# First expert's gate: two column pieces multiplied with all tokens, the place matrix scaled and in f32

## What is computed

```
def _expert_choice_ffn(xn, router_w, w_gate, w_up, w_down):
    probs = softmax(xn @ router_w)                 # 256 tokens x 16 experts
    gate, idx = top_k(probs^T, 32)                 # each expert takes its 32 best tokens
    xg = xn[idx]                                   # 16 experts x 32 tokens x 1024
    h = silu(xg @ w_gate) * (xg @ w_up)            # 1024 -> 2048
    y = (h @ w_down) * gate                        # 2048 -> 1024
    return zeros.at[idx].add(y)                    # back to the tokens
```

## Time and profile before

| | |
|---|---|
| median of three runs | 2114.65 us |
| the profiled execution | 2118.86 us |
| its span, first to last instruction | 2117.0 us |
| mean granted TensorE clock | 0.859 |
| HBM traffic, mean over the span | 348 GB/s |
| busy: PE, DVE, ACT, POOL | 77%, 35%, 21%, 15% |

### The profile page before, as it was taken

The page is one execution under the profiler, slowest core; times in us unless marked ns, Lnnn a source line. Parts: engine busy times, 40 slices in busy tenths (PEclk is TensorE's granted clock), DMA queues, the critical chain, the costliest instruction groups (busy, mean ns, idle before and its releaser), DMA issues. The chain is left out here.

```text
span 2117.0 us, 23616 instructions
## 1 busy us (share of the span) xinstructions
PE 1626.3 (77%) x9071; PEld 779.3 (37%) x9071; DVE 738.2 (35%) x1697; ACT 449.9 (21%) x992; POOL 315.6 (15%) x312
## 2 busy tenths in 40 slices
PE   7998879979777877789889766666666666766665
PEld 7987855545333333339678311111111110111110
DVE  4265267776777767654653200000000000000001
ACT  4255134222222312224531300000000000000001
POOL 0141033433433333310040000000000000000000
PEclk9998989989999999999989886778777777787777
DMA  7541389999999999986204899999999999999997
GB/s 267 170 128 61 130 327 379 419 420 421 419 421 421 420 420 421 421 340 239 110 14 174 357 420 420 419 420 420 421 421 420 420 421 421 421 420 420 421 420 313
DMA packets 111668, 737.54 MB, mean 348 GB/s; under 512 B 14048, under 2 KB 15968, under 8 KB 27616
## 3 DMA queue, kind: packets, MB, share of 16 engines
q1 hardware_dynamic: 74432, 467.86, 54.7%
q0 software_dynamic: 36864, 268.45, 30.6%
q10 hardware_dynamic: 288, 0.08, 0.0%
HBM read 735.30 MB, written 1.05 MB: 348 GB/s over the span
## 5 line engine op out<-in xcount | busy, mean ns | idle before, releaser
L2501 PE MATMUL ps<-arena,xe 128*32 128x512 f32 x2032 | 376.7, 832 | 194.2 <-DMA arena<-in_experts_in 194.2
L1123 PE MATMUL ps<-arena 128*128 128x512 f32 x820 | 404.1, 643 | 114.7 <-ACT arena L1302 114.6
L2658 DVE TENSOR_TENSOR low<-low,ps 128x512 f32<-128x512 f32 x16 | 11.0, 688 | 873.2 <-PE ps L2501 873.2
L1508 DVE CUSTOM_DVE_ANT_0 arena<-arena,ps 128x1024 f32<-128x1024 f32 x205 | 247.7, 1218 | 126.4 <-DMA arena<-in_peer,arena 126.3
L1123 PEld LDWEIGHTS ps<-arena 128*128 128x128 f32 x820 | 163.4, 205 | 336.4 <-issue 192.0
L1023 POOL DMA_INDIRECT arena<-in_peer,arena x205 | 196.2, 957 | 435.1 <-PE ps L1123 334.8
L2501 PEld LDWEIGHTS ps<-arena,xe 128*32 128x32 f32 x2032 | 47.3, 124 | 509.8 <-DMA arena<-in_experts_in 487.9
L2525 PE MATMUL ps<-arena,hT 128*32 128x512 f32 x1024 | 163.9, 743 | 78.6 <-DMA arena<-in_experts_down 67.4
L2690 POOL TENSOR_TENSOR low<-h,hT 128x512 f32<-128x512 f32 x2 | 2.5, 1270 | 933.8 <-DVE h L2671 933.8
L1302 ACT ACTIVATE arena<-ident,arena 128x128 f32<-128x128 f32 x256 | 83.7, 391 | 149.5 <-DVE arena L1518 145.2
L2525 PEld LDWEIGHTS ps<-arena,hT 128*32 128x32 f32 x1024 | 26.1, 122 | 198.9 <-DMA arena<-in_experts_down 160.7
(11 more groups left out here) (459 smaller groups left out, 1937.8 us busy)
## 6 DMA issues: line engine op xcount, KB each, us to landing
arena<-in_experts_in SPq DMA_DIRECT2D x254, 1024.0 KB, 26.9
arena<-in_experts_down SPq DMA_DIRECT2D x128, 1024.0 KB, 27.2
ring<-in_stream SPq DMA_DIRECT2D x42, 512.0 KB, 5.4
arena<-in_stream SPq DMA_DIRECT2D x36, 512.0 KB, 3.8
arena<-in_stream SPq DMA_DIRECT2D x14, 1024.0 KB, 7.1
arena<-in_peer,arena POOLq DMA_INDIRECT x205, 18.4
h<-in_x SPq DMA_DIRECT2D x1, 1024.0 KB, 5.0
arena<-in_sel SPq DMA_DIRECT2D x1, 1024.0 KB, 5.7
```

What stands on the lines that cost most here:

```text
L1123: last = nc.tensor.matmul(ps[:, 4 + 2 * t + half, :], diag[:, n % DIAGS, :], slot(n)[:, D + half * BANK:D + (half + 1) * BANK], start=firs ...
L1508: nc.vector.tensor_tensor_reduce(slot(n)[:, 0:D], slot(n)[:, 0:D], xrow(j // (QUADS // NT)), 1.0, 0.0, ALU.mult, ALU.add, act_in[:, u % 2, ...
L2501: last = nc.tensor.matmul(ps[32 * j:32 * (j + 1), 4 + r // KB, :], xe[:, k, :], w[:, j * BANK:(j + 1) * BANK], start=(k == 0), stop=(k == ...
```

## The change

Expert 0's gate matrix is partly stored in column pieces (all 1024 rows x 256 columns, as [128, 8 x 256]) in place of row pieces. The order of its pieces is now: gate column pieces 0 and 1, the eight row pieces of up, gate column pieces 2 to 7. The eight down pieces and all other experts stay as they were.

- Gate column pieces 0 and 1 are multiplied with all 256 tokens (`for_all_tokens`, from `hT`), one quarter ahead of the turn of the probabilities, three behind it. ACT copies the result (256 tokens x 512 columns) to `dense` when both pieces are used, and `open_chosen` picks expert 0's 32 rows with a product with `onehot`.
- `onehot` is f32 and holds the token's 1/rms in place of 1; `xs`, `xs_parts` and the split by ACT and POOL are gone. The gathers multiply the residual `h` itself, in f32: two products a k in place of four.
- DVE makes expert 0's 32 columns of `onehot` first (`oh_first`), PE gathers expert 0 by itself (16 products of 128x32 into bank 0), and one DVE instruction brings them to `xe`. The other 15 experts' gathers (8 x 2 products of 128x480) stand between up pieces (four) and behind gate pieces 2 to 5 (four).
- Gate column pieces 2 to 7 (`open_gate`): each is 8 products of 32 stationary and 256 moving columns, all into one column group (`j = c // 2`).
- Piece 15, still in `hT`, is now loaded behind piece 18, when two pieces are used.

```diff
             for q in range(RING3 + 2, PAIR):
                 sync.wait_ge(ring.used, ring.before(q) + 1)
+                if q == RING3 + 1 + DENSE:
+                    first_lap(RING3 - 1)
                 load(q, 0)
...
+            def for_all_tokens(c, t):
+                if t == 0:
+                    ring.arrived(pe, c)
+                w = ring.piece(c, 0).rearrange("p (k c) -> p k c", k=KB)
+                for k in range(KB):
+                    last = nc.tensor.matmul(ps[:, 2 + c, t * S:(t + 1) * S], hT[:, k, t * P:(t + 1) * P], w[:, k, :],
+                                            start=(k == 0), stop=(k == KB - 1))
+                if t == NT - 1:
+                    last.then_inc(ring.used, 1)
+
+            for_all_tokens(0, 0)
             pe.wait_ge(ex_p, 1)
...
             last.then_inc(pt_ps, 1)
+            for_all_tokens(0, 1)
+            for t in range(NT):
+                for_all_tokens(1, t)
             pe.wait_ge(rep_ready, 1)
...
+            pe.wait_ge(oh_first, NT)
+            for k in range(KB):
+                for t in range(NT):
+                    last = nc.tensor.matmul(ps[:, 0, k * CAP:(k + 1) * CAP], h[:, t, k * P:(k + 1) * P], onehot[:, t, 0:CAP],
+                                            start=(t == 0), stop=(t == NT - 1))
+            last.then_inc(x0_ps, 1)
...
                 for t in range(NT):
-                    for a in range(2):
-                        last = nc.tensor.matmul(ps[:, k % 4, :], xs_parts[:, a, t, k * P:(k + 1) * P], onehot[:, t, :],
-                                                start=(t == 0 and a == 0), stop=(t == NT - 1 and a == 1))
+                    last = nc.tensor.matmul(ps[:, k % 4, CAP:NEXP * CAP], h[:, t, k * P:(k + 1) * P], onehot[:, t, CAP:NEXP * CAP],
+                                            start=(t == 0), stop=(t == NT - 1))
                 last.then_inc(xg_ps, 1)
...
+            def open_up(k):
+                if k == 0:
+                    pe.wait_ge(xe_first, 1)
+                q = DENSE + k
+                ring.arrived(pe, q)
+                w = ring.piece(q, 0)
+                for j in range(4):
+                    last = nc.tensor.matmul(ps[32 * j:32 * (j + 1), 5, :], xe[:, k, :], w[:, j * BANK:(j + 1) * BANK],
+                                            start=(k == 0), stop=(k == KB - 1), tile_position=(0, 32 * j))
+                last.then_inc(ring.used, 1)
+
+            def open_chosen():
+                for t in range(NT):
+                    nc.tensor.matmul(ps[0:32, 4, :], onehot[:, t, 0:CAP].bitcast(F32), dense[:, t, :],
+                                     start=(t == 0), stop=(t == NT - 1), tile_position=(0, 0))
+
+            def open_gate(c):
+                q, j, half = KB + c, c // 2, c % 2
+                ring.arrived(pe, q)
+                w = ring.piece(q, 0).rearrange("p (k c) -> p k c", k=KB)
+                for k in range(KB):
+                    last = nc.tensor.matmul(ps[32 * j:32 * (j + 1), 4, half * S:(half + 1) * S], xe[:, k, :], w[:, k, :],
+                                            start=(k == 0), stop=(k == KB - 1), tile_position=(0, 32 * j))
+                last.then_inc(ring.used, 1)
...
+                    for k in range(KB):
+                        open_up(k)
+                        if k % 2 == 1:
+                            gather(k // 2)
+                    open_chosen()
+                    for c in range(DENSE, KB):
+                        open_gate(c)
+                        if c < DENSE + 4:
+                            gather(c - DENSE + 4)
```

More of the change, by code:

```diff
@@ L1694 @@
 FIRST_LOADS = 4
+DENSE = 2
 OUT_BANK, POOLED_EARLY = (6, 7, 2, 3), 2
@@ L2331, in experts @@
     low_c, over_xs, over_hT = Carve(low2), Carve(low2), Carve(hT[:, :, :].rearrange("p k s -> p (k s)"))
-    xs = low_c(NT, D)
+    low_c(2 * D)
     xg = low_c(KB, NEXP * CAP)
-    r_tile = lambda name, *shape: expert_stack.enter_context(nc.sbuf_tensor(name, [P, *shape], F32R))
-    onehot = r_tile("onehot", NT, NEXP * CAP)
-    xs_parts = r_tile("xs_parts", 2, NT, D)
+    onehot = expert_stack.enter_context(nc.sbuf_tensor("onehot", [P, NT, NEXP * CAP], F32))
     diag = expert_stack.enter_context(nc.sbuf_tensor("diag", [NEXP, NEXP, CAP], F32R))
@@ L2487, in expert @@
             def expert(pair, odd, opening=False, closing=False):
                 e = pair * 2 + odd
-                if not opening:
+                if opening:
+                    for k in range(KB):
[7 more added lines that the diff above has]
+                            gather(c - DENSE + 4)
+                    pe.wait_ge(xg_sb, KB)
+                else:
@@ L2490, in expert @@
                     pe.wait_ge(xe_ready, e)
-                for r in range(2 * KB):
+                for r in range(0 if opening else 2 * KB):
                     q = odd * PER + r
[L2494 to L2497, removed]
                     ring.arrived(pe, q, pair)
@@ L2566, in _, with hidden @@
             nc.scalar.activation(probs[:, :, :], probs[:, :, :], ACT.Exp).then_inc(ex_exp, 1)
+            act.wait_ge(ring.used, DENSE)
             for t in range(NT):
-                nc.scalar.activation(xs[:, t, :], h[:, t, :], ACT.Copy, scale=rms[:, 1, t:t + 1]).then_inc(xs_all, 1)
-                act.wait_ge(xs_all, t + 1)
-                nc.scalar.activation(xs_parts[:, 0, t, :], xs[:, t, :], ACT.Copy).then_inc(xs_high, 1)
+                nc.scalar.activation(dense[:, t, :].rearrange("p (c s) -> p c s", c=DENSE), ps[:, 2:2 + DENSE, t * S:(t + 1) * S],
+                                     ACT.Copy).then_inc(dense_sb, 1)
             for k in range(KB):
                 act.wait_ge(xg_ps, k + 1)
[L2573 to L2576, removed]
+                nc.scalar.activation(xg[:, k, CAP:NEXP * CAP], ps[:, k % 4, CAP:NEXP * CAP], ACT.Copy, scale=T.gains[:, 3, k:k + 1]).then_inc(xg_sb, 1)
+            def hidden(e, gate_pieces):
+                act.wait_ge(ring.used, used(gate_pieces, e))
                 nc.scalar.activation(sg, ps[:, 4, :], ACT.Silu).then_inc(sg_ready, 1)
@@ L2582, in _ @@
                     nc.scalar.activation(yb[:, half * BANK:(half + 1) * BANK], ps[:, 6 + half, :], ACT.Copy).then_inc(y_ready, 1)
+            hidden(0, 2 * KB)
+            with act.Fori(1, NEXP) as e:
+                hidden(e, KB)
             nc.scalar.activation(ssq[:, 6:7], tokid[:, 0:1], ACT.Sqrt)
@@ L2646, in _, with places @@
             dve.wait_ge(bc_ps, 1)
+            def places(t, slots, done):
+                nc.vector.tensor_scalar(onehot[:, t, slots], ps[:, 7, slots], tokid[:, t:t + 1], rms[:, 1, t:t + 1],
+                                        ALU.is_equal, ALU.mult).then_inc(done, 1)
             for t in range(NT):
-                nc.vector.tensor_scalar(onehot[:, t, :], ps[:, 7, :], tokid[:, t:t + 1], None, ALU.is_equal).then_inc(oh_ready, 1)
+                places(t, slice(0, CAP), oh_first)
+            for t in range(NT):
+                places(t, slice(CAP, NEXP * CAP), oh_ready)
             dve.wait_ge(cols_ps, 1)
[L2650 to L2653, removed]
+            link(nc.vector.tensor_copy(cols[:, :, :], ps[:, 6, 0:2 * NEXP].rearrange("p (a e) -> p a e", a=2)))
+            dve.wait_ge(x0_ps, 1)
+            nc.vector.tensor_tensor(xe[:, :, :], ps[:, 0, 0:KB * CAP].rearrange("p (k c) -> p k c", k=KB),
+                                    T.gains[:, 3, :].unsqueeze(2).broadcast_to([P, KB, CAP]), ALU.mult).then_inc(xe_first, 1)
+            dve.wait_ge(xg_sb, KB)
             def body(e, last_one):
@@ L2764, in host_arrays @@
     out["experts_in"] = np.stack([f["expert_w_gate_2"][0].reshape(NEXP, KB, P, PW), f["expert_w_up_2"][0].reshape(NEXP, KB, P, PW)], axis=1)
+    opening = out["experts_in"][0].reshape(2 * KB, P, PW).copy()
+    by_cols = col_pieces(f["expert_w_gate_2"][0, 0])
+    opening[0:DENSE], opening[DENSE + KB:] = by_cols[0:DENSE], by_cols[DENSE:]
+    opening[DENSE:DENSE + KB] = out["experts_in"][0, 1]
+    out["experts_in"][0] = opening.reshape(2, KB, P, PW)
     out["experts_down"] = (f["expert_w_down_2"][0].reshape(NEXP, 4, 4, P, 2, BANK).transpose(0, 4, 2, 3, 1, 5)
```

15 lines of the change are left out of this document (7 added, 8 removed).

## The result

The changed kernel took 2131.26 us, median of 4 runs (2127.08 to 2134.94), against 2115.38 us for the kernel before (4 runs). The ratio is 1.007, 95% interval 1.0057 to 1.0083: 12 to 18 us slower. Forecast were 2130 us and +15.1.

What follows compares the result with a forecast made beforehand. The expert stage's weight stream was taken as the bound, so the end moves by lost DMA time: 22.2 us against 7.1 before, +15.1. 2114.65 + 15.1 = 2129.8, say 2130 us; range 2122 to 2148.

Steps and rivals of the forecast that it cites:

- Two dates, of which the 17th use decides: Opening: first used pieces against 1178, 17th used piece against 1211.4; the 17th, forecast at 1233.6, sets 22.2 us lost.
- All tokens: Opening: four quarters of f32 products with all tokens, 64 records, 14.0 us, plus 0.40 for the turn; DVE's search hidden.
- Spread, first places, own gather: Behind the last quarter: spread 0.45, two compares 0.18 each, own gather 3.6, copy 0.48 and handovers; `xe` ready at 1185.6.
- Up pieces: Expert 0's eight up row pieces, 8 x 8 records: 7.0 us.
- Other gathers: Eight f32 gathers for the other 15 experts: 13.1 us, plus 3.2 for layout changes at 0.4 each.
- Picking the 32 rows: Four 512-column records right ahead of gate piece 2, in another column group: 0 us by overlap, bound 1.7.
- Gate pieces 2 to 7: Six late column pieces, each 16 records in one column group: 3.5 us a piece, 21.0 in all, the largest term.
- Rival C: Gate pieces overlap at 0.87 us each, 15.8 us less in all; the end moves -0.7, no change; chance 0.08.
- Sum to the last gate piece: From `xe` ready through up pieces, gathers, picking and gate pieces: 44.3 us, ending at 1229.9.
- Rival A: Clock falls to 1.2 GHz in the gate pieces: total +22 for the last two, +36 for all six; chance 0.20.
- Rival B: The gate pieces' 96 weight loads stand open, 10.8 us more, total about +26; chance 0.04.
- The hole: 8 to 11 us of empty DMA around 1225 to 1235, piece 32's load waiting for the first down piece.

Runs made afterwards that it cites:

- e3: Changed kernel with two more 1 MB places for the first lap of loads; stage 968.0 us, ratio 1.0066 to the kernel before.
- e1: Changed kernel with the six late gate pieces packed over three column groups, same bytes; stage 954.0 us, ratio 1.0014 to the kernel before.
- e5: e1 with the other experts' eight gathers moved behind expert 0's down pieces; stage 949.1 us, ratio 1.0006 to the kernel before.
- e2: Changed kernel with only 1 of 8 products for each late gate piece, all loads kept; stage 953.5 us, ratio 1.0008 to the kernel before.
- e7: e5 plus two more 1 MB places, and the token-number spread ahead of the last all-token quarter; stage 944.6 us, ratio 0.9974 to the kernel before.
- e4: Kernel before with only the f32 gathers and expert 0's places and gather first; stage 954.6 us, ratio 1.0033 to the kernel before.

## Why the prediction was right

- *The bound.* The kernel is as long as its weight stream, and the end moves by the change in lost DMA time: 15.4 us by the bytes, 14.5 by the stage, 15.1 forecast. Shown by all 13 profiles: the stage is the lost time plus 941.6 to 944.4.
- *Two dates, of which the 17th use decides.* Shown: e3 fills the early hole and gains nothing, e1 makes the 17th use 11.9 earlier and the stage 11.5 shorter, and e5 finds the floor (18.0 earlier than e1 for 4.9 us).
- *How close, and luck.* The mechanism is right, but a hit within 0.6 us is partly luck. The 17th use was 1.5 us later than forecast (69.1 for 67.6), and by the prediction's own sum (its date less 52.4) this would have made +16.6; the end moved 14.5. The step from the date to the end was thus some 2 us off the other way, as it is in the other late kernels (1 to 3 us), and where these lie no run shows. The early losses, 4.9 in the forecast, are 6.8 us by the bytes (1170 to 1190), which moves nothing while the 17th use is late.
- *All tokens.* Forecast 14.4 with the turn, measured 3.55 + 0.22 + 10.36 = 14.13; clock 1.00 all along, DVE's search hidden. Piece 18 went out before the stream was dry.
- *Spread, first places, own gather.* L2481's start to the first up product: 5.39 measured, 5.15 forecast.
- *Up pieces.* Forecast 7.0, measured 3.31 + 3 x 1.85 = 8.9. This was mis-sized: I took the full clock because PE doesn't idle for long, but it fell to 0.50 for 3.4 us right there. A longer fall is part of why e2 and e3 missed their expectations.
- *Other gathers.* 8 x 1.81 = 14.5 with all layout changes, forecast 16.3. In e5, back to back and without a change of layout, the eight take 13.09, forecast 13.1. So it was the 0.4 us for each change that was too much: it is 0.17 in the gather, plus under 0.1 in the pieces beside it.
- *Picking the 32 rows* took nothing, as forecast: with gate piece 2 it is 3.59, a gate piece alone 3.57. PE's timeline has the two groups in turn:

```profile
1195.39 0.62 PE L2519 MATMUL ps<-low,onehot 128*32 128x512 f32 x1
1195.41 0.62 PE L2527 MATMUL ps<-arena,xe 128*32 128x256 f32 x2
1195.85 0.59 PE L2519 MATMUL ps<-low,onehot 128*32 128x512 f32 x1
1195.86 0.59 PE L2527 MATMUL ps<-arena,xe 128*32 128x256 f32 x2
```

- *Gate pieces 2 to 7.* Forecast 21.0, measured 3.59 + 3 x 3.57 + 7.04 = 21.3. The 0.117 us of a lone half of 64 columns carried over to a lone group of 32. Rival C is refuted.
- *Sum to the last gate piece* from `xe`: 44.3 forecast, 44.7 measured; the errors above cancel. The tail was 1.2 us longer than summed, since the first down pieces met the half clock.
- *Rival A*: the clock stayed at 1.00 from 1184 to 1226, though four of the six gate pieces alternate with gathers over the full array; only the last two, 7.04 us, had a quarter of the columns at work without a break. *Rival B*: 16 records in 3.57 us leave no room for open weight loads of 0.11 each; they were hidden. The trace does not agree with the sentence of the Trainium skill that the prediction weighed ("TensorE: Matmul & The Clock Gate", Part 3, "The mechanism").
- *The hole.* Forecast 8 to 11 us of empty DMA between 1225 and 1235 in the old time base; it is 9 us, 60 to 69 us behind the logits, which is 1226 to 1235 there.

## What to carry to other kernels

A ring with extra places for its first lap has more than one deadline: write down for each load which use it waits for, and look for the step where the wanted count jumps (here from 14 to 17). Where that use is already late, work that is put ahead of it costs its full time even in a stage where PE has a third of its time free, and before that date is met, a deeper buffer or an earlier first use buys nothing; once it is met, two places of 1 MB bought 4.6 us. Column pieces for narrow stationaries were dear here because neighbouring products went to one column group (3.57 us a piece; 1.83 and less when they were packed over three).

## What the runs showed of the hardware

- A lone column group of 32 streams no faster than the full array: 16 records of 256 columns in 3.57 us, where L2420 has 3.50 for as many. The granted clock stayed at 1.00 through the last two such pieces, 7.04 us without a break.
- Four f32 products of 512 columns took 0.9 us in four column groups (half of 1.85), and 1.83 us in three with a full-array gather on either side (e1).
- By the starts in the timeline, PE begins a later matmul of another column group alongside earlier ones that still wait for their own group: L2527's records start 0.02 us behind L2519's first, though three more of L2519 stand ahead of them in the program.
- 32 weight loads of 128 columns with 32 moving columns each took 3.5 us at the 2.4 GHz level (e7) and 7.05 at 1.2 (e4). Around this stretch the granted clock fell in nine of eleven profiles that came to it at 1.00, though PE counts as busy nearly throughout.
